# Two more weight slots for the second mixture of experts, laid over dead buffers, and its transfers in the order in which slots come free

## What is computed

```python
def hier_moe(h, w_group, b_group, w_expert, b_expert, w_gate, w_up, w_down):
    ...
    g_prob = jax.nn.softmax(hf @ w_group.astype(F32) + b_group.astype(F32), axis=-1)
    g_idx = jnp.argmax(g_prob, axis=-1)
    ...
    top_p, top_i = lax.top_k(e_prob, TOP_K_EXPERTS)
    ...
    out = jnp.zeros(hf.shape, F32)
    for e in range(N_EXPERTS_2):
        hid = jax.nn.silu(t @ w_gate[e]) * (t @ w_up[e])
        out = out + combine[:, e:e + 1] * (hid @ w_down[e]).astype(F32)
    return out.reshape(bsz, seq, d).astype(h.dtype)
```

## Time and profile before

| | before |
|---|---|
| median of three runs | 2322.46 us (2321.23 to 2323.91) |
| the profiled execution | 2310.58 us |
| its span in the trace | 2308.8 us |
| TensorE busy | 1839.7 us (80% of the span) |
| VectorE busy | 811.2 us (35%) |
| ScalarE busy | 496.6 us (22%) |
| moved by DMA | 713.56 MB, mean 309 GB/s |

### The profile page before, as it was taken

The page is one execution under the profiler, slowest core; times in us unless marked ns, Lnnn a source line. Parts: engine busy times, 40 slices in busy tenths (PEclk is TensorE's granted clock), DMA queues, the critical chain, the costliest instruction groups (busy, mean ns, idle before and its releaser), DMA issues. The chain is left out here.

```text
span 2308.8 us, 28283 instructions
## 1 busy us (share of the span) xinstructions
PE 1839.7 (80%) x11518; PEld 837.9 (36%) x11518; DVE 811.2 (35%) x1618; ACT 496.6 (22%) x1005; POOL 76.8 (3%) x96
## 2 busy tenths in 40 slices
PE   7899998888989988789977788689968656555555
PEld 3655545433333333333333333354524422222221
DVE  2224332333433334433344334687682300000001
ACT  2032301222222133332333333321301200000000
POOL 0000000000000000000000000291000000000000
PEclk9999999899999999999999999799989777777778
DMA  8745268498797699999999999432126399999996
GB/s 287 268 146 181 93 215 310 176 398 329 328 388 318 278 424 408 422 424 376 406 423 423 423 417 420 143 117 103 40 73 236 122 426 428 428 427 427 425 424 260
DMA packets 113956, 713.56 MB, mean 309 GB/s; under 512 B 16703, under 2 KB 21006, under 8 KB 68654
## 3 DMA queue, kind: packets, MB, share of 16 engines
q1 hardware_dynamic: 105344, 704.98, 75.3%
q10 hardware_dynamic: 8398, 5.47, 0.8%
HBM read 709.35 MB, written 1.07 MB: 308 GB/s over the span
## 5 line engine op out<-in xcount | busy, mean ns | idle before, releaser
L779 PE MATMUL ps<-ring,ar 128*32 128x512 f32 x3072 | 374.5, 627 | 50.2 <-DMA ring<-in_w 21.7
L434 PE MATMUL ps<-ar 128*128 128x128 f32 (+5 forms) x1750 | 357.9, 361 | 41.9 <-PEq L691 13.4
L441 PE MATMUL ps<-ring,ar 128*32 128x512 f32 x1536 | 211.5, 713 | 192.1 <-DMA ring<-in_w_up 81.0
L434 PEld LDWEIGHTS ps<-ar 128*128 128x128 f32 (+2 forms) x1750 | 235.9, 201 | 165.8 <-issue 111.1
L434 PE MATMUL ps<-ring,ar 128*128 128x512 f32 (+2 forms) x624 | 262.9, 581 | 18.0 <-DVE ar L1855 9.9
L779 PEld LDWEIGHTS ps<-ring,ar 128*32 128x32 f32 x3072 | 99.8, 113 | 318.9 <-issue 275.8
L1610 DVE TENSOR_SCALAR ar<-ps 128x256 f32<-128x256 f32 x128 | 54.4, 425 | 432.2 <-PE ps L779 425.5
L790 PE MATMUL ps<-ring,ar 128*32 128x512 f32 x1536 | 175.2, 595 | 21.7 <-ACT ar L2207 21.7
L441 PEld LDWEIGHTS ps<-ring,ar 128*32 128x32 f32 x1536 | 60.6, 129 | 337.0 <-issue 336.1
L434 PEld LDWEIGHTS ps<-ring,ar 128*128 128x128 f32 x624 | 119.2, 193 | 156.4 <-issue 135.6
L538 PE MATMUL ps<-ring,ar 128*128 128x512 f32 x384 | 172.4, 598 | 3.4 <-ACT ar L2038 3.4
(11 more groups left out here) (393 smaller groups left out, 1290.5 us busy)
## 6 DMA issues: line engine op xcount, KB each, us to landing
ring<-in_w SPq DMA_DIRECT2D x192, 2048.0 KB, 18.4
ring<-in_w_gate SPq DMA_DIRECT2D x32, 2048.0 KB, 17.8
ring<-in_w_up SPq DMA_DIRECT2D x32, 2048.0 KB, 16.8
ring<-in_w_down SPq DMA_DIRECT2D x32, 2048.0 KB, 16.3
ring<-in_w_in SPq DMA_DIRECT2D x21, 2048.0 KB, 8.1
ring<-in_w_ada SPq DMA_DIRECT2D x12, 2048.0 KB, 8.6
ring<-in_w_out SPq DMA_DIRECT2D x4, 2048.0 KB, 8.1
ring<-in_w_branch SPq DMA_DIRECT2D x6, 1024.0 KB, 5.0
```

The costliest lines, as they stand in the source:

```text
L434: ins = self.t.e.matmul(o, l, r, start=(i == 0), stop=(i == len(pairs) - 1))
L441: ins = self.t.e.matmul(b[32 * i:32 * i + 32, :], l, r, start=(k == 0), stop=(k == len(steps) - 1))
L779: ins = e.matmul(b[32 * s:32 * s + 32, :], HG[:, 2 * c + r, 32 * n:32 * n + 32], W[:, r, HALF(s)], start=False, stop=(c == 3 and r == 1))
```

## The change

The constant `NSLOT` goes from 7 to 9, and `RING`, the slots within `ring`, stays 7. Slots 7 and 8 are cut from `ar`: slot 7 is the 4096 elements from `GMo`, slot 8 those from 6736 to 10832. What the second mixture keeps in `ar` is packed below 6736 or moved to `small`, and the products of the dense part reach their slots in another order.

```diff
-NSLOT = 7
+NSLOT = 9
+RING = 7
...
     def RG_(i, off, *shape):
         n = int(np.prod(shape))
+        if i >= RING:
+            return A(MORE[i - RING] + off, *shape)
         return cut(ring[:, i * SLOT + off:i * SLOT + off + n], shape)
...
+    MORE = (GMo, 6736)
...
-    AC2 = A(4096, 512)
+
+    AT2, AC2, YG2 = A(2048, 4, 128), A(3072, 512), A(3584, 1024)
+    SB2 = [A(4608 + 256 * i, 2, 128) for i in range(2)]
+    SWB2 = A(5120, 1, 2, 128)
+    SWT2 = [A(5376 + 256 * i, 1, 256) for i in range(2)]
+    SG2 = A(5888, 512)
...
-    W36, B36 = A(9216, 8, 36), A(9504, 36)
+    W36, B36 = A(2512, 8, 36), A(2800, 36)
...
-        for n in (2, 1):
-            for h in range(2):
-                up(n, h)
-        fetch(("glu",), kpn(a["w_glu_2"][0]), 4, 512, lane=d2)
-        for h in range(2):
-            up(0, h)
-        for h in range(2):
-            fetch(("wo", 2, h), kpn(a["w_out_2"][0])[:, :, HALF(h)], 8, 512, lane=d2)
-
-
+
+        up(2, 0, (1,))
+        up(2, 1, (2,))
+        up(1, 0, (0,))
+        q.wait_ge(s_pe, pe["pv", 2, 11])
+        fetch(("glu",), kpn(a["w_glu_2"][0]), 4, 512, lane=(7,))
+        up(1, 1, (1,))
+        up(0, 0, (2,))
+        up(0, 1, (0,))
+        units = [(nm, u, i) for u in range(NE // 4) for nm in ("w_gate_2", "w_up_2", "w_down_2") for i in range(4)]
+        lanes = (3, 4, 5, 6, 8, 2, 0, 1, 7)
         q.wait_ge(s_pe, pe["sy", 3])
-        for u in range(NE // 4):
-            for nm, r in (("w_gate_2", 8), ("w_up_2", 8), ("w_down_2", 4)):
-                for i in range(4):
-                    if (u, nm, i) == (0, "w_gate_2", 3):
-                        q.wait_ge(s_dve, dve["branch", 2, 0])
-                    fetch((nm, u, i), a[nm][0, 4 * u + i].rearrange("(p r) n -> p r n", r=r), r, SLOT // r,
-                          lane=(3, 4, 5, 6, 0, 1, 2))
+        for k, (nm, u, i) in enumerate(units):
+            if k == 3:
+                out2(0, (1,))
+                out2(1, (7,))
+                q.wait_ge(s_dve, dve["branch", 2, 0])
+            if k == 4:
+                q.wait_ge(s_pe, pe["up", 0, 1, 1])
+            r = 4 if nm == "w_down_2" else 8
+            fetch((nm, u, i), a[nm][0, 4 * u + i].rearrange("(p r) n -> p r n", r=r), r, SLOT // r,
+                  lane=(lanes[k % 9],))
...
             s.wait_ge(s_pe, pe["at2", u])
-            if u > 1:
-                s.wait_ge(s_pe, pe["l2_2", u - 2, 1])
-            act["at2", u] = s(s.own.activation(ATB[u % 2][:, 0:4, :],
+            if u > 0:
+                s.wait_ge(s_pe, pe["l2_2", u - 1, 1])
+            act["at2", u] = s(s.own.activation(AT2,
```

More of the change, by code:

```diff
@@ L233, in build @@
     TM = [A(9216 + 768 * i, 768) for i in range(2)]
-    AC2 = A(4096, 512)
+    AT2, AC2, YG2 = A(2048, 4, 128), A(3072, 512), A(3584, 1024)
[3 more added lines that the diff above has]
+    SG2 = A(5888, 512)
     B1R = A(HT, 2048, part=(0, 32))
     L, E, E2 = A(10000, 2, 32), A(10064, 2, 40), A(10144, 2, 40)
-    TOP, NM, SM = A(10224, 2, 8), A(10240, 2), A(10242, 2)
-    CT, SEL = A(10256, 256, part=(0, 32)), A(10512, 2, 32)
+    TOP, NM, SM = A(10224, 2, 8), small[:, 104:106], small[:, 106:108]
+    CT, SEL = A(10256, 256, part=(0, 32)), [A(10512, 2, 32), A(2872, 2, 32)]
     AT = [A(2048 * i, 8, 256) for i in range(2)]
@@ L269, in build @@
     NJ = A(7168, 2048)
-    W36, B36 = A(9216, 8, 36), A(9504, 36)
-    L36, E16, R16 = A(10000, 2, 36), A(10072, 2, 16), A(10104, 2, 16)
-    T8, GS2, GG = A(10136, 2, 8), A(10152, 2), A(10154, 2)
-    E40, R40, EX = A(10160, 2, 40), A(10384, 2, 40), A(10320, 2, 32)
+    W36, B36 = A(2512, 8, 36), A(2800, 36)
+    L36, E16, R16 = A(2048, 2, 36), A(2120, 2, 16), A(2152, 2, 16)
+    T8, GS2, GG = A(2184, 2, 8), A(2200, 2), A(2202, 2)
+    E40, R40, EX = A(2208, 2, 40), A(2432, 2, 40), A(2368, 2, 32)
     w_in, w_in2 = kpn(a["w_in"][0]), kpn(a["w_in_2"][0])
@@ L372, in sync, with up, out2 @@
         got["bc"] = k
[L374 removed]
+        def up(n, h, lane):
             w = (a["w_up_ssm_2"], a["w_up_dsa_2"], a["w_up_mem_2"])[n][0]
[L376 removed]
+            fetch(("up", n, h), kpn(w)[:, :, HALF(h)], 4, 512, lane=lane)
+        def out2(h, lane):
+            fetch(("wo", 2, h), kpn(a["w_out_2"][0])[:, :, HALF(h)], 8, 512, lane=lane)
         for c in range(6):
             fetch(("gate", 2, c), w_in2[:, :, 1988 + 512 * c:2500 + 512 * c], 8, 512, lane=d2)
[L380 to L397 removed]
+        up(2, 0, (1,))
[8 more added lines that the diff above has]
+        lanes = (3, 4, 5, 6, 8, 2, 0, 1, 7)
+        q.wait_ge(s_pe, pe["sy", 3])
+        for k, (nm, u, i) in enumerate(units):
[8 more added lines that the diff above has]
+                  lane=(lanes[k % 9],))
         sync_past2(q)
@@ L708, in tensor_route @@
         t.wait_ge(s_c2, 16)
-        w.sums(b[:, 0:32], [(upper, SEL[:, 0, :])])
-        w.sums(b[:, 32:64], [(upper, SEL[:, 1, :]), (ones, SEL[:, 0, :])])
-        pe["rk", m] = w.sums(b[:, 64:96], [(ones, SEL[:, 0, :]), (ones, SEL[:, 1, :])])
+        s0, s1 = (SEL[m - 1][:, tb, :] for tb in range(2))
+        w.sums(b[:, 0:32], [(upper, s0)])
+        w.sums(b[:, 32:64], [(upper, s1), (ones, s0)])
+        pe["rk", m] = w.sums(b[:, 64:96], [(ones, s0), (ones, s1)])
     def gather(t, w, m, u, lane):
@@ L1006, in tensor_moe2 @@
         for u in range(NE // 4):
-            HG, AT_ = HGB[u % 2], ATB[u % 2]
+            HG, AT_ = HGB[u % 2], AT2
             rows = [slice(32 * i, 32 * i + 32) for i in range(4)]
@@ L1502, in vector_ranks @@
     def vector_ranks(v, m, cap):
-        v(v.own.tensor_scalar(SEL, CMB, 0.0, None, ALU.not_equal))
+        v(v.own.tensor_scalar(SEL[m - 1], CMB, 0.0, None, ALU.not_equal))
         dve["sel", m] = v.n
@@ L1511, in vector_ranks @@
         v(v.own.tensor_tensor(CO_, CO_, CMB, ALU.mult))
-        v(v.own.scalar_tensor_tensor(out=RK, in0=rk, scalar=1.0, in1=SEL, op0=ALU.add, op1=ALU.mult))
+        v(v.own.scalar_tensor_tensor(out=RK, in0=rk, scalar=1.0, in1=SEL[m - 1], op0=ALU.add, op1=ALU.mult))
         v(v.own.tensor_scalar(RK, RK, -1.0, None, ALU.add))
@@ L1539, in vector_select @@
             four = [z[:, :, 4 * u:4 * u + 4].unsqueeze(3).to_broadcast([128, 2, 4, 32]) for z in (RK, CMB)]
-            S = SB[u % 2].rearrange("p b (x s) -> p b x s", x=4)
+            S = SB2[u % 2].rearrange("p b (x s) -> p b x s", x=4)
             v(v.own.tensor_tensor(S, iota[:, 0:32].unsqueeze(1).unsqueeze(1).to_broadcast([128, 2, 4, 32]), four[0],
                                   ALU.is_equal))
-            k = v(v.own.tensor_tensor(SWB[:, 0].rearrange("p b (x s) -> p b x s", x=4), S, four[1], ALU.mult))
+            k = v(v.own.tensor_tensor(SWB2[:, 0].rearrange("p b (x s) -> p b x s", x=4), S, four[1], ALU.mult))
         dve["sel", m, u] = k
@@ L1930, in vector_moe2 @@
         for u in range(NE // 4):
-            sg = TM[0][:, 0:512]
+            sg = SG2
             v.wait_ge(s_act, act["sg2", u])
@@ L2297, in scalar_dense2 @@
         scalar_mt(s, 2)
+        e.dma_start(W36[:, :, 0:4], kpn(a["w_group_2"][0])).then_inc(s_r2, 16)
+        e.dma_start(W36[:, :, 4:36], kpn(a["w_expert_2"][0])).then_inc(s_r2, 16)
+        e.dma_start(B36[:, 0:4], a["b_group_2"][0:1, :].partition_broadcast(128)).then_inc(s_r2, 16)
+        e.dma_start(B36[:, 4:36], a["b_expert_2"][0:1].rearrange("o g e -> o (g e)").partition_broadcast(128)
+                    ).then_inc(s_r2, 16)
+        got["rt", 2] = 64
         for tb in range(2):
```

21 lines of the change are left out of this document (8 added, 13 removed).

## The result

The median of six runs is 2309.74 us (2298.51 to 2311.22), that of six runs of the kernel before beside them 2322.94 us. The ratio is 0.9932 with a 95% interval of 0.9911 to 0.9954: 0.7% faster, more than the 0.43% of the forecast. The ratio is not the quotient of the two medians. That is 0.9943, which would give 2309.3 us, within the range. The quotient of the two means is 0.9932. The means differ from the medians by the two short runs of the six, 2298.51 and 2301.82 us. The profiled execution took 2298.51 us, its span is 2296.7 us, 12.1 us less than before.

The account below looks back on a forecast made before the run. The prediction took the second mixture's end to be bound by tiles not fitting the slots, arriving at the DMA's pace. Two fewer at 4.929 us save 9.9 us: 2322.46 - 9.9 = 2312.6 us, range 2308.0 to 2317.5.

Parts of the forecast that it names:

- What bounds the end: Second mixture: from the first gate group's end, all tiles that did not fit the slots follow at 4.929 us each.
- two fewer remain: When the first gate group ends, 87 tiles are left and not 89: 9.9 us less.
- The places of all issues: SP's new queue ahead of the second mixture: nine tiles issued before 1800 us, the tenth at 1843.7.
- no landing between the first gate and up groups: Second mixture's start: the up group has all four tiles, waits for no landing and ends near 1852 us.
- rival C: `w_out_2` lands late for `tensor_out`: costs from 9 us late, cancels the gain at 18.9 us late; chance 0.03.
- rival A: Second mixture's stream: nine slots lower the DMA rate; 1% costs 4.3 us (2316.9), 2.3% the whole gain; chance 0.10.
- the last of the sum and its range: Whole kernel: 9.9 us off the 2322.46 us median gives 2312.6 us, range 2308.0 to 2317.5.
- rival D: End of kernel: dips close (2 us) and the last down group takes 7.11 us: 14.5 us off, 2308.0; chance 0.03.
- what a measurement of this kernel can tell: Whole kernel: 0.2% of 2322 us, 4.6 us, is about what a measurement can tell from no change.
- The 11.9 us: Whole kernel: the runs' median stands 11.9 us above the profiled execution, a difference carried over to the forecast.
- ScalarE's issues: Ahead of ScalarE's squares: four small transfers moved into 14.82 us of idling, issues taking 2.2 us, costing nothing.
- rival B: ScalarE's small transfers land too late for the logits, each packet waiting for a tile row: 91 us, kernel 2367; chance 0.04.

Follow-up runs that it names:

- short kernels: Kernel before, changed kernel and its seven-slot version, each without 30 of 32 first-mixture experts and the second mixture's fallback: medians 1342.27, 1332.45 and 1342.21 us.
- nine-slot kernels: Changed kernel, its repeat, and a version issuing no mixture tile until half the output product is done: ratios to the kernel before 0.9932, 0.9942, 0.9951.
- the first comparison: Six runs of the changed kernel beside six of the kernel before: medians 2309.74 and 2322.94 us, ratio 0.9932.
- the full stream: Changed kernel with ScalarE's four small transfers issued once more into dead space behind the evictions of u = 3, tiles always queued; one run, 2303.76 us.

## Why the prediction was right and where it was wrong

**Right, by its own steps.** What bounds the end (the tiles that do not fit, at 4.93 us each) and that two fewer remain: short kernels 9.8 us, forecast 9.9 (that they lie so close is partly luck, given the interval of 2.7 us). The places of all issues, nine tiles in time, no landing between the first gate and up groups, 1881.58 for the next gate group (1881.8), 2274.82 for the last landing (2275.7): all as written, the issues to 2 us and the rest to 1 us. `w_out_2` was in time (rival C did not happen: `tensor_out` starts 2.27 us behind its transposes, as in the earlier trace rows). The rate did not fall with nine slots (rival A did not happen): 428 GB/s.

**Wrong: the scatter under the forecast.** The step that failed is the last of the sum and its range. I set the forecast against the median of three runs that lay within 1.5 us of it and took these 1.4 us as the scatter. The range's lower end, 2308.0, is rival D alone, a sum of small gains, with nothing for the comparison. I had priced what a measurement of this kernel can tell at 4.6 us myself and did not use it there. Later sets of the kernel before ran from 2311.07 to 2327.66 us within one set of 26 runs, and the first mixture alone moved by 13 us between profiles. A median of six runs can therefore lie 3 us from the change's own effect, and most likely did: 13.2 us (15.8 by the ratio) against 9.8 in the short kernels. The two runs of the six that pull the ratio down, 2298.51 and 2301.82 us, are those with the highest granted clocks (0.920 and 0.918, the others 0.913 to 0.916). The 11.9 us between the profiled execution and the median of the runs should have warned me: it was a sample of this scatter, one execution that ran short, and I carried it over as a constant. The range held what the change does and not what a comparison of it shows.

**Mis-sized: ScalarE's issues.** I took 2.2 us from issues onto an idle queue; they took 12, because the third was held for 9.58. Of the 16.9 us between the first of them and ScalarE's squares 4.9 were left, so it still cost nothing. The hold ended here as the tiles' transfers ran out. If it ends with them, then two more tiles queued at that moment would have made the squares some 5 us late, and these stand on the chain (an estimate from two tiles of 4.93 us and the 4.9 us left; no run shows it). I had written rival B down for the landing of these transfers; the first thing to be late would have been the engine that issues them.

**Left open.** Whether the medians of nine-slot kernels in full length lie 1 to 3 us under the effect by more than scatter is not settled; the granted clock of the six runs of the kernel before in the first comparison is not known, so they cannot be compared at equal clock. The intervals (0.9932, 0.9942 and 0.9951, each about 0.0023 to either side) hold an effect of 10 us, 0.9957, in two of three cases; the first misses it by 0.0003.

## What to carry to other kernels

Where a stage streams weights at the DMA's limit and a stage ahead of it leaves the DMA idle, the price of a slot is one tile's transfer time, and it does not matter when a tile is issued as long as it is there; look for dead buffers even for a single use, and split the last tiles so that little work stands behind the last landing. A small transfer with many tiny pieces beside such a stream needed one large row's time for each piece that falls to a DMA engine, and held the engine that issued it. A forecast of 0.4% needs the scatter of the unchanged stages in its range; cutting such a stage short in both kernels brought the difference out to 2 or 3 us with five runs each, and the profiles' stretches bring single steps out to some tenths of a us.

## What the runs showed that I had not expected

A DMA issue on ScalarE took 9.58 us, and 35.89 us in the full stream, where it takes 0.4 to 0.7 otherwise; the two issues ahead of it had put 2048 small pieces into its queue, and tiles were moving beside them. What sets such an issue free stays open. The first mixture took 1138.4 to 1151.8 us in ten profiles of kernels whose instructions are the same there, and the time of a run goes with its granted clock.
